# Per-head channel sums of an RWKV-7/HGRN2 layer as two rounded products instead of one float32 product, with the first tile's evacuation moved

## The chip, the cores and the metric

One Trainium2 chip, one NeuronCore. The metric is the device time of one execution in microseconds. The engines are TensorE (PE, with PEld for its weight loads), VectorE (DVE), ScalarE (ACT), GpSimd (POOL) and the DMA queues that SyncE (SP) issues.

## The reference

A trunk of two layers on 512 tokens of width 1024, all in float32. The change touches only the first ("even") layer, whose projection `z = h @ w_in` feeds eight HGRN2 heads of width 128 and sixteen RWKV-7 heads of width 64. Four values in it are sums over the channels of a head:

```
o  = rmsnorm(hgrn2(q, f, i))                      # mean of o*o over 128 channels
kk = k * k_k;  kk = kk / max(norm(kk), 1e-12)     # sum of kk*kk over 64 channels
y  = (y - mean(y)) * rsqrt(mean((y-mean(y))**2) + eps)   # sum of squares over 64 channels
y  = y + sum(r * k * r_k, -1) * v                 # the "bonus": sum over 64 channels
```

Then the outputs are gated, projected and added, and the second ("odd") layer (block attention and an RG-LRU) and a final norm follow.

## The kernel before

Channels lie on the 128 partitions and tokens along the free axis, so a tile of z is 128 x 512. Everything is written by hand for each engine, with semaphores between them.

The even layer runs in rounds. Round i projects eight tiles, `t(0)` to `t(7)`, that belong to HGRN2 head i and to the pair of RWKV-7 heads i. A tile is eight accumulated steps of 128 channels, and each step is three rounded (float32r) products, `split_products`: high weights by high input, high by low, low by high. A tile takes two weight units; POOL splits each unit into `w_hi` (line 352) and `w_lo` (line 354) into one of four slots (`split_unit`) once TensorE has left the slot (`units_done`). The tiles alternate between PSUM banks 0 and 1, and a bank must be emptied (`free0`, `free1`) before the tile after next starts in it; `gated(i, 0, ...)` on VectorE (line 1908) empties tile 0 by multiplying it with its sigmoid (`sig_q`, by ScalarE).

Between the tiles of round i TensorE computes HGRN2 head i (`hg_level`, `hg_diagonal`, `hg_keys`, `hg_changes`, `hg_outputs`) and the RWKV-7 pair r = i-1, whose tiles came in the round before. The pair starts with `low_rank(r)` at the head of the round; then, among `t(0)` and `t(1)`, stand the four channel sums: `key_norm(r)` and `hg_norm(r)` after the first half of `t(0)`, `head_var(r-1)` after its second half, `bonus(r)` after the first half of `t(1)`. Each is one float32 product of a 128 x 128 matrix of ones (`ones`) or of two 64 x 64 blocks of ones (`bones`) with a 128 x 512 operand:

```
mm(R0[:, :], bones, t1).then_inc(sem["rw_ssq"], 1)
```

After `t(2)` come `products(r)`, `turned_products(r)`, two `token_rows`, and the blockwise triangular inverse (`inverse_pt`, `inverse_n`), which runs between parts of `t(3)`.

VectorE's list at the head of round i is: `decay_sums(r)`, `key_norm(r)` (line 1990, a clamp of the sum, `rw_m1`), `operands(r)` (which waits for ScalarE's inverse root of it, `rw_rn`, and for the two exponentials), `read_operands(r)` (lines 2010 and 2011), `gated(i, 0)`, `head_norm`, `head_gate`, `pair_norm`, `pair_gain`, `pair_gate` (of pair r-1), `bonus`, then two tensor_scalars for the forget gates (lines 2158, 2159), `level(i, 0)`, `gated(i, 2)`, and the masked copies `strict` and `inverse_start` (line 1901), which `inverse_pt(r, 1, 0)` on TensorE waits for. Pair norm, gain and gate exist from round 2 on. `last_round` does the last pair (r = 7) between the embedding's and the output projection's tiles.

## Time and profile before

| | |
|---|---|
| median of 3 runs | 1178.47 us (1177.82 to 1179.08) |
| the profiled execution, its own time | 1178.48 us |
| its span in the trace | 1176.7 us |
| PE busy | 1144.8 us, 97% |
| DVE busy | 772.9 us, 66% |
| POOL busy | 635.8 us, 54% |
| ACT busy | 448.4 us, 38% |

The profiled execution lies on the median, and 1.8 us of its time are outside the span. The granted TensorE clock is 0.998 of full speed. Busy shares are means over the program: where an engine waits is read from its timeline. Matmuls overlap, so the time of one in a row of instructions is read from start to start.

### The profile page before, as it was taken

What the parts mean: (1) busy time and instruction counts of PE and PEld (TensorE: products, weight loads), DVE (VectorE), ACT (ScalarE), POOL (GpSimd) and SP (SyncE); (2) the same over time, 40 slices, a digit from 0 to 9 for tenths busy, and PEclk for the clock granted to TensorE, in tenths of its full rate; (3) what the DMA queues carried; (4) which work ended last, traced back from release to release, by engine and by line L of the source; (5) the groups of instructions that cost most, each with busy time, mean ns of one, the idle gap of its engine ahead of it and who ended that gap; (6) DMA issues with size and microseconds to landing.
All of it is one profiled execution on the core that took longest, in us unless ns stands there. A gap on an engine that the chain in (4) does not pass through costs nothing.

```text
span 1176.7 us, 31072 instructions
## 1 busy us (share of the span) xinstructions
PE 1144.8 (97%) x12076; PEld 906.7 (77%) x12076; DVE 772.9 (66%) x1350; ACT 448.4 (38%) x848; POOL 635.8 (54%) x594
## 2 busy tenths in 40 slices
PE   7899999999999999999999999999999999999996
PEld 4678877877788788777887778888777777778884
DVE  7874684675566756846755542539968686967647
ACT  5452343343433423433335420226234444352224
POOL 5553452443444534524435557777847475749872
PEclk9999999999999999999999999999999999999999
DMA  5221121211221212202212143333323232323331
GB/s 199 73 68 53 55 66 39 66 55 38 66 56 46 66 48 64 66 30 66 57 46 72 57 135 116 91 99 90 99 64 89 72 89 63 89 63 96 101 90 72
DMA packets 46890, 87.38 MB, mean 74 GB/s; under 512 B 5824, under 2 KB 7104, under 8 KB 46656
## 3 DMA queue, kind: packets, MB, share of 16 engines
q1 hardware_dynamic: 44496, 81.04, 23.6%
q10 hardware_dynamic: 2288, 4.72, 1.3%
q8 instruction: 91, 1.49, 0.5%
q14 instruction: 15, 0.12, 0.0%
HBM read 83.65 MB, written 2.10 MB: 73 GB/s over the span
## 4 chain that ended last, share of the span: by engine, by line
PE 86%; DVE 7%; issue 2%; ACT 1%; DVEq 0%; ACTq 0%
PE psum L398 83%; PE psum L1081 1%; DVE mix L1792 1%; DVE h_split L2399 1%; PE psum L552 1%; DVE y L1792 1%; ACT mix L1210 1%; DVE h_split L1792 1%; DVE mix L2578 0%; DVE psum L2335 0%; PE psum L714 0%; PE psum L550 0%; DVE mix L2343 0%; DVE mix L2574 0%; DVE psum L2350 0%
## 5 line engine op out<-in xcount | busy, mean ns | idle before, releaser
L398 PE MATMUL psum<-h_split,w_hi 128*128 128x512 f32 x2320 | 748.9, 404 | 14.0 <-DVE h_split L1792 9.0
L398 PEld LDWEIGHTS psum<-h_split,w_hi 128*128 128x128 f32 x2320 | 421.7, 188 | 118.2 <-issue 31.9
L352 POOL TENSOR_SCALAR w_hi<-w_raw 128x512 fp32r<-128x512 f32 x290 | 215.9, 745 | 480.5 <-PE psum L398 337.0
L398 PE MATMUL psum<-h_split,w_lo 128*128 128x512 f32 x1160 | 454.2, 392 | 0.0
L354 POOL TENSOR_TENSOR w_lo<-w_raw,w_hi 128x512 fp32r<-128x512 f32 x290 | 408.6, 1409 | 24.2
L398 PEld LDWEIGHTS psum<-mix 64*64 64x64 f32 (+3 forms) x8256 | 228.9, 138 | 69.1 <-issue 49.1
L1210 ACT ACTIVATE mix<-psum 128x512 f32<-128x512 f32 (+4 forms) x289 | 138.9, 494 | 368.9 <-PE psum L398 235.6
L398 PE MATMUL psum<-mix 64*64 64x64 f32 (+5 forms) x8256 | 269.6, 236 | 4.5 <-issue 2.6
L398 PEld LDWEIGHTS psum<-h_split,w_lo 128*128 128x128 f32 x1160 | 218.0, 188 | 48.2 <-issue 0.7
L1210 ACT ACTIVATE mix<-mix 128x512 f32<-128x512 f32 (+3 forms) x256 | 131.3, 546 | 119.8 <-DVE mix L2316 49.1
L1901 DVE COPY_PREDICATED mix<-mask,psum 128x128 f32<-128x128 uint8 (+1 forms) x192 | 82.0, 469 | 43.8 <-PE psum L398 41.5
L1210 ACT ACTIVATE mix<-psum,mix 128x512 f32<-128x512 f32 (+3 forms) x88 | 53.3, 630 | 98.4 <-PE psum L398 69.3
L1792 DVE SCALAR_TENSOR_TENSOR mix<-mix 128x512 f32<-128x512 f32 (+1 forms) x112 | 77.0, 688 | 14.9 <-ACT mix L1210 11.7
L1792 DVE SCALAR_TENSOR_TENSOR mix<-psum,mix 128x64 f32<-128x64 f32 (+1 forms) x80 | 37.3, 467 | 55.1 <-ACT mix L1210 46.0
L2050 DVE COPY mix<-psum 128x128 f32<-128x128 f32 (+1 forms) x80 | 25.5, 318 | 57.9 <-PE psum L398 57.6
L1210 ACT ACTIVATE h_split<-y 128x512 fp32r<-128x512 f32 x44 | 25.5, 627 | 69.9 <-PE psum L398 69.5
L398 PE MATMUL psum<-mix,fconst 128*128 128x512 f32 x92 | 45.4, 597 | 0.1
L1936 DVE TENSOR_TENSOR mix<-mix 128x256 f32<-128x256 f32 x56 | 36.1, 644 | 0.1
L2316 DVE TENSOR_TENSOR mix<-mix,psum 128x512 f32<-128x512 f32 x16 | 10.9, 679 | 24.8 <-PE psum L398 24.8
L1939 DVE TENSOR_TENSOR mix<-mix 128x256 f32<-128x256 f32 x56 | 27.0, 482 | 0.0
L2242 DVE TENSOR_TENSOR h_split<-y,h_split 128x512 fp32r<-128x512 f32 x10 | 11.5, 1206 | 23.4 <-ACT h_split L1210 23.4
L1796 DVE TENSOR_TENSOR h_split<-mix,h_split 128x512 fp32r<-128x512 f32 x16 | 18.6, 1163 | 12.4 <-ACT h_split L1210 12.4
(139 smaller groups left out, 709.7 us busy)
## 6 DMA issues: line engine op xcount, KB each, us to landing
w_raw<-wall SPq DMA_DIRECT2D x290, 256.0 KB, 2.6
mix<-xT SPq DMA_DIRECT2D x4, 512.0 KB, 7.1
mix<-xT ACTq DMA_DIRECT2D x1, 2048.0 KB, 8.1
out<-mix SPq DMA_DIRECT2D x7, 256.0 KB, 2.5
mix<-pT ACTq DMA_DIRECT2D x2, 512.0 KB, 3.9
mix<-lru_w ACTq DMA_DIRECT2D x4, 256.0 KB, 3.3
mix<-w2a ACTq DMA_DIRECT2D x16, 32.0 KB, 2.3
mask<-mask_u SPq DMA_DIRECT2D x1, 432.0 KB, 7.4
```

The source lines that it names most:

```text
L352: pool.tensor_scalar(w_hi[:, slot, :, :], w_raw[:, slot, :], 1.0, 0.0, ALU.mult, ALU.add).then_inc(sem["w_hi"], 1)
L354: pool.tensor_tensor(w_lo[:, slot, :, :], w_raw[:, slot, :], w_hi[:, slot, :, :].bitcast(F32).rearrange("p k n -> p (k n)"), ALU.subtract) ...
L398: return pe.matmul(o, lhsT, rhs, start=start, stop=stop, skip_group_check=True)
L552: last = pe.transpose(o[:, at], (b_t if n == 1 else k_t)[:, at], ident)
L1081: last = pe.transpose(bank[4][:, j * L:(j + 1) * L], prob[:, n % 2, j * L:(j + 1) * L], ident)
L1210: return act.activation(o, i, func, bias=bias, scale=scale, **kw)
L1792: return dve.scalar_tensor_tensor(out=o, in0=a, scalar=scalar, in1=b, op0=op0, op1=op1)
L1796: dve.tensor_tensor(h_split[:, KC + c, :], hn[:, c % 2, :], h_split[:, c, :].bitcast(F32), ALU.subtract).then_inc(sem["h_ready"], 1)
L1901: return dve.copy_predicated(dst, mask, src)
L1936: dve.tensor_tensor(q_dst, q_src, t_even.to_broadcast([P, nb, m]), ALU.mult)
L1939: dve.tensor_tensor(k_dst, k_src, t_odd.to_broadcast([P, nb, m]), ALU.mult)
L2050: dve.tensor_copy(dst, src).then_inc(sem["rw_pb"], 1)
```

## The change

It does these things:

- All four sums, in all eight pairs, become two rounded products each (`sum_products`): the operand's high half, rounded by ScalarE on its way into `sum_split`, and the low half, which POOL makes by a subtraction (`key_low`, `output_square_low`, `bonus_low`, `variance_low`). The variance and the bonus of the last pair stay single float32 products.
- ScalarE computes three of the operands twice, once in float32 and once rounded, and copies the fourth (`bonus_high`).
- `key_norm` moves on TensorE and on VectorE into the round before (after the first half of `t(7)`, and after the masked copies), and the logarithm and exponential behind it (`key_scale`) move on ScalarE ahead of the two decay exponentials.
- `gated(i, 0)` on VectorE moves ahead of `read_operands`.
- In `last_round` the output's sum moves between the two halves of the last tile.
- POOL's weight loop is unrolled to a whole round, with the subtractions at fixed places. One conversion of the constants (128 x 256) is added at the start.
- To make room, `t2`, `n_add`, `s_all` and `osig` share memory with other tiles, and two semaphores go.

```diff
+        sum_split = sb("sum_split", [P, 2, 2, T], F32R)
+        sum_const = sb("sum_const", [P, 2, P], F32R)
+        ones_r, bones_r = sum_const[:, 0, :], sum_const[:, 1, :]
...
-        t1, t2, w_a = (place(T) for _ in range(3))
+        t1, w_a = (place(T) for _ in range(2))
+        t2 = kr[:, 0, :]
...
-        n_add = place(T).rearrange("p (c t) -> p c t", c=RC)
-        s_all = place(T).rearrange("p (c t) -> p c t", c=RC)
+        n_add = k_t.rearrange("p (c t) -> p c t", c=RC)
+        s_all = b_t.rearrange("p (c t) -> p c t", c=RC)
...
+            def key_low(r):
+
+                pool.wait_ge(sem["sum_hi"], count("sum_hi", r, 0))
+                pool.tensor_tensor(sum_split[:, 0, 1, :], t1, sum_split[:, 0, 0, :].bitcast(F32), ALU.subtract).then_inc(sem["sum_lo"], 1)
...
+            def bonus_low(r):
+
+                pool.wait_ge(sem["sum_hi"], count("sum_hi", r, 2))
+                pool.tensor_tensor(sum_split[:, 0, 1, :], t2, sum_split[:, 0, 0, :].bitcast(F32), ALU.subtract).then_inc(sem["sum_lo"], 1)
+
+            def variance_low(r):
+
+                pool.wait_ge(sem["rw_dsq"], count("rw_dsq", r))
+                pool.tensor_tensor(sum_split[:, 1, 1, :], y_sq, sum_split[:, 1, 0, :].bitcast(F32), ALU.subtract).then_inc(sem["dsq_lo"], 1)
+
+            pool.wait_ge(const_loaded, 64)
+            pool.tensor_scalar(sum_const[:, :, :], fconst[:, 1:3, :], 1.0, 0.0, ALU.mult, ALU.add)
+
+            groups = 2 * TILES // SLOTS
...
+            key_low(0)
+            with pool.Fori(1, EV_ROUNDS) as i:
+                for g in range(groups):
+                    for slot in range(SLOTS):
+                        split_unit(i * groups + g, slot)
+                        if g == 0 and slot == 3:
+                            output_square_low(i - 1)
+                        elif g == 1 and slot == 0:
+                            bonus_low(i - 1)
+                        elif g == 3 and slot == 2:
+                            variance_low(i - 1)
+                key_low(i)
+            g_prj = (U_PRJ0 + 2) // SLOTS
+            for g in range(groups * EV_ROUNDS, g_prj):
+                for slot in range(SLOTS):
+                    split_unit(g, slot)
+            output_square_low(EV_ROUNDS - 1)
...
+            def sum_products(o, of, pair):
+
+                mm(o, of, sum_split[:, pair, 0, :], True, False)
+                return mm(o, of, sum_split[:, pair, 1, :], False, True)
+
             def low_rank(r):
                 pe.wait_ge(w2_loaded, (r + 1) * 32)
+                pe.wait_ge(sem["rw_m1"], count("rw_m1", r))
...
             def key_norm(r):
-                pe.wait_ge(sem["rw_ksq"], count("rw_ksq", r))
-                pe.wait_ge(sem["rw_sw"], count("rw_sw", r))
-                mm(R0[:, :], bones, t1).then_inc(sem["rw_ssq"], 1)
+                pe.wait_ge(sem["sum_lo"], count("sum_lo", r, 0))
+                sum_products(R0[:, :], bones_r, 0).then_inc(sem["rw_ssq"], 1)
 
             def head_var(r):
-                pe.wait_ge(sem["rw_dsq"], count("rw_dsq", r))
                 if isinstance(r, int) and r == EV_ROUNDS - 1:
+                    pe.wait_ge(sem["rw_dsq"], count("rw_dsq", r))
                     pe.wait_ge(sem["rw_s"], count("rw_s", r, 5))
+                    last = mm(R1[:, :], bones, y_sq)
                 else:
+                    pe.wait_ge(sem["dsq_lo"], count("dsq_lo", r))
                     pe.wait_ge(sem["rw_av"], count("rw_av", r + 1))
-                mm(R1[:, :], bones, y_sq).then_inc(sem["rw_var"], 1)
+                    last = sum_products(R1[:, :], bones_r, 1)
+                last.then_inc(sem["rw_var"], 1)
 
             def bonus(r):
-                pe.wait_ge(sem["rw_rk"], count("rw_rk", r))
-                pe.wait_ge(sem["rw_m1"], count("rw_m1", r))
-                mm(R0[:, :], bones, t2).then_inc(sem["rw_bon"], 1)
+                if isinstance(r, int) and r == EV_ROUNDS - 1:
+                    pe.wait_ge(sem["rw_rk"], count("rw_rk", r))
+                    pe.wait_ge(sem["rw_sw"], count("rw_sw", r))
+                    last = mm(R0[:, :], bones, t2)
+                else:
+                    pe.wait_ge(sem["sum_lo"], count("sum_lo", r, 2))
+                    pe.wait_ge(sem["rw_sw"], count("rw_sw", r))
+                    last = sum_products(R0[:, :], bones_r, 0)
+                last.then_inc(sem["rw_bon"], 1)
...
             def hg_norm(r):
-                pe.wait_ge(sem["hg_sq"], count("hg_sq", r))
-                mm(H0[:, :], ones, hk).then_inc(sem["hg_ssq"], 1)
+                pe.wait_ge(sem["sum_lo"], count("sum_lo", r, 1))
+                sum_products(H0[:, :], ones_r, 0).then_inc(sem["hg_ssq"], 1)
...
                 if pair:
-                    key_norm(r)
                     hg_norm(r)
                 t(0, 4, KC)
...
                 t(7, 0, 4)
+                key_norm(i)
                 hg_level(i, 6)
...
                 low_rank(r)
-                part_tile(EV_ROUNDS, 3, 0, KC)
-                key_norm(r)
+                part_tile(EV_ROUNDS, 3, 0, 4)
                 hg_norm(r)
+                part_tile(EV_ROUNDS, 3, 4, KC)
                 head_var(r - 1)
                 bonus(r)
...
             def out_squares(r):
                 act.wait_ge(sem["rw_yc"], count("rw_yc", r))
-                f(by_parity(y_sq.rearrange("p (c t) -> p c t", c=RC)),
-                  psum[:, 2:4, 256:512].rearrange("p g (c t) -> p g c t", c=4), ACT.Square).then_inc(sem["rw_dsq"], 1)
+                last = f(by_parity(y_sq.rearrange("p (c t) -> p c t", c=RC)),
+                         psum[:, 2:4, 256:512].rearrange("p g (c t) -> p g c t", c=4), ACT.Square)
+                if isinstance(r, int) and r == EV_ROUNDS - 1:
+                    last.then_inc(sem["rw_dsq"], 1)
+                else:
+                    if not is_first(r):
+                        act.wait_ge(sem["rw_var"], count("rw_var", r - 1))
+                    f(by_parity(sum_split[:, 1, 0, :].rearrange("p (c t) -> p c t", c=RC)),
+                      psum[:, 2:4, 256:512].rearrange("p g (c t) -> p g c t", c=4), ACT.Square).then_inc(sem["rw_dsq"], 1)
+
+            def key_scale(r):
+                act.wait_ge(sem["rw_m1"], count("rw_m1", r))
+                f(t1, t1, ACT.Ln).then_inc(sem["rw_ln"], 1)
+                act.wait_ge(sem["rw_ln"], count("rw_ln", r))
+                f(t1, t1, ACT.Exp, bias=bias[:, 2:3], scale=-0.5).then_inc(sem["rw_rn"], 1)
+
+            def bonus_high(r):
+                act.wait_ge(sem["rw_rk"], count("rw_rk", r))
+                act.wait_ge(sem["hg_ssq"], count("hg_ssq", r))
+                f(sum_split[:, 0, 0, :], t2, ACT.Copy).then_inc(sem["sum_hi"], 1)
...
                     act.preload_act_table_set("natural_log_exp_and_others")
+                    key_scale(r)
                     act.wait_ge(sem["rw_prep"], count("rw_prep", r, 0))
                     f(e_neg[:, :, 1:RL + 1], cum[:, :, 1:RL + 1], ACT.Exp, scale=KAPPA).then_inc(sem["rw_exp"], 1)
                     act.wait_ge(sem["rw_exp"], count("rw_exp", r, 0))
                     f(e_pos, cum, ACT.Exp, scale=-KAPPA).then_inc(sem["rw_exp"], 1)
                     if is_first(r):
                         decay_rates()
-                    act.wait_ge(sem["rw_m1"], count("rw_m1", r))
-                    f(t1, t1, ACT.Ln).then_inc(sem["rw_ln"], 1)
-                    act.wait_ge(sem["rw_ln"], count("rw_ln", r))
-                    f(t1, t1, ACT.Exp, bias=bias[:, 2:3], scale=-0.5).then_inc(sem["rw_rn"], 1)
+                    bonus_high(r)
                     act.wait_ge(sem["hg_ssq"], count("hg_ssq", r))
...
                 act.wait_ge(sem["free1"], freed(i, 5))
-                f(t1, wk, ACT.Square, scale=cur_e[:, K_K:K_K + 1]).then_inc(sem["rw_ksq"], 1)
+                f(t1, wk, ACT.Square, scale=cur_e[:, K_K:K_K + 1])
+                if pair:
+                    act.wait_ge(sem["rw_bon"], count("rw_bon", r))
+                f(sum_split[:, 0, 0, :], wk, ACT.Square, scale=cur_e[:, K_K:K_K + 1]).then_inc(sem["sum_hi"], 1)
...
                 f(hk, H1[:, :], ACT.Square).then_inc(sem["hg_sq"], 1)
+                act.wait_ge(sem["rw_ssq"], count("rw_ssq", i))
+                f(sum_split[:, 0, 0, :], H1[:, :], ACT.Square).then_inc(sem["sum_hi"], 1)
...
                     decay_sums(r)
-                    key_norm(r)
                     operands(r)
+                    gated(i, 0, "sig_q", sig_b, hq)
                     read_operands(r)
...
-                gated(i, 0, "sig_q", sig_b, hq)
+                if not pair:
+                    gated(i, 0, "sig_q", sig_b, hq)
...
                 masked(i, 7)
+                key_norm(i)
                 states(i)
```

VectorE at the head of a round from round 2 on, before. The `mix` tiles are all working tiles in SBUF; L1792 is a helper (scalar_tensor_tensor), L1990 is the clamp of the key sum, L2010 and L2011 are the read operands, L1908 is tile 0's evacuation; ISA and REGISTER_ALU rows are bookkeeping.

```order
184 L1792 SCALAR_TENSOR_TENSOR mix<-mix 128x512 [waits rw_prep]
185 L1990 TENSOR_SCALAR mix<-psum 128x512 [waits rw_ssq]
186 L1792 SCALAR_TENSOR_TENSOR mix<-mix 128x512 [waits rw_rn]
187 L2001 ISA
188 L1792 SCALAR_TENSOR_TENSOR mix<-mix 128x512 [waits rw_kk]
189 L2003 REGISTER_ALU
190 L2004 TENSOR_TENSOR mix<-mix 128x512 [waits rw_exp]
191 L2006 TENSOR_TENSOR mix<-mix 128x512 [waits rw_kk]
192 L2010 TENSOR_TENSOR mix<-mix 128x512
193 L2011 TENSOR_TENSOR mix<-mix 128x512
194 L1908 TENSOR_TENSOR mix<-psum,mix 128x512 [waits sig_q]
195 L1792 SCALAR_TENSOR_TENSOR mix<-psum,mix 128x512 [waits hg_rstd]
```

The same place in the change, where every line is 77 or 78 further down (L1869 is the helper, L2087 and L2088 the read operands, L1985 the evacuation).

```order
186 L1869 SCALAR_TENSOR_TENSOR mix<-mix 128x512 [waits rw_prep]
187 L1869 SCALAR_TENSOR_TENSOR mix<-mix 128x512 [waits rw_rn]
188 L2078 ISA
189 L1869 SCALAR_TENSOR_TENSOR mix<-mix 128x512 [waits rw_kk]
190 L2080 REGISTER_ALU
191 L2081 TENSOR_TENSOR mix<-mix 128x512 [waits rw_exp]
192 L2083 TENSOR_TENSOR mix<-mix 128x512 [waits rw_kk]
193 L1985 TENSOR_TENSOR mix<-psum,mix 128x512 [waits sig_q]
194 L2087 TENSOR_TENSOR mix<-mix 128x512
195 L2088 TENSOR_TENSOR mix<-mix 128x512
196 L1869 SCALAR_TENSOR_TENSOR mix<-psum,mix 128x512 [waits hg_rstd]
```

The clamp is gone from this place, and the evacuation with its wait for `sig_q` now stands ahead of the read operands; all that was behind it stands as it did.

ScalarE at the head of a round, before, from the first activation after its table load (L1210 is the helper for all activations) to the sigmoid of tile 0 (the last row).

```order
114 L1210 ACTIVATE mix<-mix 128x8x64 [waits rw_prep]
115 L1381 ISA
116 L1210 ACTIVATE mix<-mix 128x520 [waits rw_exp]
117 L1210 ACTIVATE mix<-mix 128x512 [waits rw_m1]
118 L1210 ACTIVATE mix<-mix,bias 128x512 [waits rw_ln]
119 L1210 ACTIVATE mix<-psum,bias 128x512 [waits hg_ssq]
120 L1210 ACTIVATE mix<-mix 128x512 [waits hg_ln]
121 L1210 ACTIVATE mix<-psum,bias 128x512 [waits rw_var]
122 L1210 ACTIVATE mix<-mix 128x512 [waits rw_lnv]
123 L1216 ISA
124 L1210 ACT_TABLE_LOAD
125 L1210 ACTIVATE mix<-psum 128x512 [waits units_done]
```

And in the change (the helper is L1269), up to the bookkeeping row ahead of the table load for the same sigmoid.

```order
119 L1269 ACTIVATE mix<-mix 128x512 [waits rw_m1]
120 L1269 ACTIVATE mix<-mix,bias 128x512 [waits rw_ln]
121 L1457 ISA
122 L1269 ACTIVATE mix<-mix 128x8x64 [waits rw_prep]
123 L1459 ISA
124 L1269 ACTIVATE mix<-mix 128x520 [waits rw_exp]
125 L1269 ACTIVATE sum_split<-mix 128x512 [waits hg_ssq,rw_rk]
126 L1269 ACTIVATE mix<-psum,bias 128x512 [waits hg_ssq]
127 L1269 ACTIVATE mix<-mix 128x512 [waits hg_ln]
128 L1269 ACTIVATE mix<-psum,bias 128x512 [waits rw_var]
129 L1269 ACTIVATE mix<-mix 128x512 [waits rw_lnv]
130 L1275 ISA
```

The pair of activations that waits for `rw_m1` now stands first, and one copy into `sum_split` is added behind the decay exponentials.

## Rows read from the trace of the kernel before

All groups but the first and the last are of round 5 of the even layer (pair 4), a round like every one from round 2 on.

**Rows 1.** The page, busy time, share and instructions of each engine.

```profile
PE 1144.8 (97%) x12076; PEld 906.7 (77%) x12076; DVE 772.9 (66%) x1350; ACT 448.4 (38%) x848; POOL 635.8 (54%) x594
```

**Rows 2.** Timeline, PE, around the channel sum `hg_norm`: start us, us, what.

```profile
400.81 0.40 PE L398 MATMUL psum<-h_split,w_lo 128*128 128x512 f32 x1
...
401.04 1.02 PE L398 MATMUL psum<-mix,fconst 128*128 128x512 f32 x2
...
402.37 0.39 PE L398 MATMUL psum<-h_split,w_lo 128*128 128x512 f32 x1
...
403.06 0.39 PE L398 MATMUL psum<-h_split,w_lo 128*128 128x512 f32 x1
```

**Rows 3.** Timeline, PE: `key_norm` with `hg_norm`, `products`, `inverse_pt`.

```profile
396.59 1.88 PE L398 MATMUL psum<-mix,fconst 128*128 128x512 f32 x4
...
413.81 2.66 PE L398 MATMUL psum<-mix 64*64 64x128 f32 x72
...
416.83 2.57 PE L398 MATMUL psum<-mix 64*64 64x64 f32 x128
```

**Rows 4.** Timeline, ACT, head of round 5: start, duration, idle before and releaser.

```profile
392.77 0.60 ACT L1210 ACTIVATE mix<-psum 128x512 f32<-128x512 f32 x1 [0.79 <-PE psum L398]
...
393.89 0.69 ACT L1210 ACTIVATE mix<-psum,mix 128x512 f32<-128x512 f32 x1 [0.52 <-PE psum L398]
...
395.21 1.28 ACT L1378 ACT_TABLE_LOAD   x1
...
396.51 1.30 ACT L1210 ACTIVATE mix<-mix 128x512 f32<-128x512 f32 x2
...
398.74 0.63 ACT L1210 ACTIVATE mix<-mix 128x512 f32<-128x512 f32 x1 [0.94 <-DVE mix L1990]
...
402.11 0.69 ACT L1210 ACTIVATE mix<-psum,bias 128x512 f32<-128x512 f32 x1 [0.73 <-PE psum L398]
...
404.77 0.60 ACT L1210 ACTIVATE mix<-psum 128x512 f32<-128x512 f32 x1
```

**Rows 5.** Timeline, DVE, head of round 5.

```profile
398.03 0.68 DVE L1990 TENSOR_SCALAR mix<-psum 128x512 f32<-128x512 f32 x1
...
400.16 1.48 DVE L1792 SCALAR_TENSOR_TENSOR mix<-mix 128x512 f32<-128x512 f32 x2 [1.46 <-ACT mix L1210]
...
402.58 1.78 DVE L2006 TENSOR_TENSOR mix<-mix 128x512 f32<-128x512 f32 x1
...
404.28 0.68 DVE L2010 TENSOR_TENSOR mix<-mix 128x512 f32<-128x512 f32 x1
...
405.49 0.68 DVE L1908 TENSOR_TENSOR mix<-psum,mix 128x512 f32<-128x512 f32 x1
...
406.97 1.00 DVE L1971 TENSOR_TENSOR y<-mix 128x512 f32 x1
...
412.01 1.64 DVE L2158 TENSOR_SCALAR mix<-mix 128x512 f32<-128x512 f32 x1
...
415.28 1.96 DVE L1901 COPY_PREDICATED mix<-mask,psum 128x256 f32<-128x256 uint8 x5
```

**Rows 6.** Timeline, POOL, head of round 5.

```profile
396.95 0.62 POOL L352 TENSOR_SCALAR w_hi<-w_raw 128x512 fp32r<-128x512 f32 x1 [3.62 <-PE psum L398]
...
402.20 1.61 POOL L354 TENSOR_TENSOR w_lo<-w_raw,w_hi 128x512 fp32r<-128x512 f32 x1
...
412.07 1.29 POOL L354 TENSOR_TENSOR w_lo<-w_raw,w_hi 128x512 fp32r<-128x512 f32 x1
```

**Rows 7.** Timeline, POOL and ACT, near tile 5 of round 5.

```profile
450.37 0.62 POOL L352 TENSOR_SCALAR w_hi<-w_raw 128x512 fp32r<-128x512 f32 x1 [2.83 <-PE psum L398]
...
456.19 0.72 ACT L1210 ACTIVATE mix<-mix 128x512 f32<-128x512 f32 x1
```

**Rows 8.** Timeline, PE: tile 2 of round 1, and `products` of the last round.

```profile
87.61 0.72 PE L398 MATMUL psum<-h_split,w_hi 128*128 128x512 f32 x2 [0.18 <-DVE mix L1908]
...
649.72 2.66 PE L398 MATMUL psum<-mix 64*64 64x128 f32 x72 [0.69 <-ACT mix L1210]
```

37 lines of the change are left out of this document (18 added, 19 removed).

## The prediction

> **What bounds the kernel now.** I read the page's busy line first: TensorE is busy 97% of the span, no other engine above 66% [rows 1]. So the span moves if TensorE has less to do, or if it must wait. The busy line can't say which, because the sums that shrink stand at the head of a round, where other engines feed TensorE. So I read, second, TensorE's timeline around one sum, to price it, and third the timelines of ScalarE, VectorE and GpSimd over the head of round 5, to see when each hands over and how far TensorE is from waiting. The reader is to see in them that TensorE has no gap there today, and that the first work to arrive close to TensorE's need is VectorE's masked copies, with under a microsecond to spare. The profiled execution took 1178.48 us (span 1176.7, 1.8 outside it), 0.01 from the median of the runs, so sums are made against 1178.5.
>
> **Price of a sum.** From the low-weight product ahead of `hg_norm` to the next one behind it, 400.81 to 402.37, is 1.56 us. That stretch holds the sum and one ordinary step of three products, and the next step takes 402.37 to 403.06, 0.69, or 0.23 a product [rows 2]. So the float32 sum costs 1.56 - 0.69 = 0.87 us, and its two rounded products 0.46: each sum gives back 0.41. Thirty of the thirty-two change (8 key, 8 output, 7 variance, 7 bonus): 30 x 0.41 = 12.3 us of TensorE work. The Trainium skill, FP8 and Floating Point Precision, TensorE Precision Notes, says that true float32 is four passes through the array; at four times 0.23 the sum would cost 0.92, and the gain would be 13.8. The row is the measurement, and the sum here goes by 0.87.
>
> Where this work lies matters. At the head of rounds 2 to 7 TensorE loses a whole key sum (0.87) and three times 0.41: 2.1 us. At the head of round 1 there is no variance: 0.87 + 0.82 = 1.69. In the last round the bonus stays, so 0.87 + 0.82 = 1.69 too. In exchange the key sum's two products are added in `t(7)` of eight rounds: 8 x 0.46 = 3.7 us. TensorE has no gap there to hide them.
>
> **Where TensorE would wait: `inverse_pt(r, 1, 0)`.** Today TensorE starts `products` at 413.81 and `inverse_pt` at 416.83 [rows 3]. The latter needs VectorE's first `strict` and `inverse_start`, the first two of the five masked copies that start at 415.28 and take 1.96 together [rows 5]; by their share I put the first two at 0.75 with the semaphore, 416.03. TensorE has 0.8 us to spare. With 2.1 us taken out ahead of it, it would arrive at 414.7, 1.3 before today's copies. So what the head of the round gives depends on how early the copies can come.
>
> ScalarE first. Its last square of the output starts at 392.77, and then it idles 0.52 for `low_rank` until 393.89; the added rounded square (as the first, 0.6) fits in that idle time but for under 0.1 [rows 4]. Sigmoids and the table load stay. The logarithm and exponential of the key sum move from 398.74 to the end of the load, 396.51, because the clamp is now a round old; the two decay exponentials (1.30 for both) follow. So the 0.94 us that ScalarE idled for the clamp is gone, and so is the 0.73 that it idled for `head_var`, which now comes with TensorE 1.7 us earlier [rows 4]. Against these stand `bonus_high`, a copy of 0.6, and the late start. Sum: 0.94 + 0.73 - 0.60 - 0.04 = 1.0 earlier, so the sigmoid of tile 0 moves from 404.77 to about 403.7, done at 404.35 [rows 4].
>
> VectorE next. It loses the clamp at 398.03 (0.68) and the idle 1.46 behind it [rows 5]. `operands`, which today run from 400.16 to 404.28 (4.1 us), then run from about 398.05 to 402.2. The evacuation of tile 0 needs the sigmoid and starts at 404.4. So VectorE idles some 2 us with the read operands (404.28 to 405.49, 1.2 us) behind the waiting instruction, where today they fill such time. From the evacuation to the masked copies VectorE takes 415.28 - 405.49 = 9.8 us today [rows 5]; now the read operands come on top: 404.4 + 9.8 + 1.2 = 415.4. That is 0.15 later than today, though everything ahead of it came earlier. Tile 0's bank is free by 405.1, and `t(2)` needs it at 413.81 - 2.1 less eight steps of 0.69, 406.2: no wait there [rows 2, 3].
>
> **GpSimd's part in it.** An SBUF-only instruction of VectorE that meets a GpSimd one is held: the operand multiply at 402.58 took 1.78 and ended 0.55 after GpSimd's subtraction (402.20 to 403.81), where the read operand at 404.28, with GpSimd idle, took 0.68; the forget gate at 412.01 took 1.64 across one of 1.29 [rows 5, 6]. The 9.8 us hold several of these, and the two read operands today hold none. With one more subtraction (`bonus_low`, 1.3 to 1.6 us, after the copy at about 399.8) ahead of the weight splits, and splits asked for earlier, the read operands would run into a split: at best 0, at worst about 0.9 in sum (each half a microsecond late). Copies then start 0.15 to 1.0 us after today's 415.28; nothing excludes either end, and I take the middle, 0.55. The Trainium skill, SBUF — State Buffer, Who interferes with whom, states the rule: a VectorE instruction with two SBUF inputs contends with a GpSimd instruction that reads SBUF, and whichever came first holds the other for its whole length. The trace agrees (402.58). By that rule alone each of the 31 added subtractions could hold VectorE by up to 1.3 us; most of them fall where VectorE has idle time.
>
> TensorE's saving at such a head is then 0.8 - 0.55 = 0.25 us instead of 2.1.
>
> **Sum.** Key products in eight rounds: +3.7. Round 1, where the pair norm, gain and gate do not exist yet and VectorE's list is three instructions shorter: the full -1.69, and the 0.18 that TensorE waited for tile 0's bank goes too [rows 8]: -1.9. Rounds 2 to 7: 6 x -0.25 = -1.5. Last round: today TensorE waits 0.69 for ScalarE's evacuation of an embedding tile ahead of `products` [rows 8]; that tile itself comes 1.7 earlier, and ScalarE's list is 1 us or more shorter ahead of it, so the whole -1.7. Total: 3.7 - 1.9 - 1.5 - 1.7 = -1.4 (the three fixed terms leave +0.1), so 1177.1 us. With copies at +0.15 it is 3.9 - 0.1 = 3.8 off (1174.7), with +1.0 it is 1.3 on (1179.8): this case's own range.
>
> **Edits at nothing.** The second squares of the variance and of the keys (0.6 and 0.7) push the next level copies on ScalarE by 1.3, which has waits for TensorE of that size behind them; without that cover it would be VectorE's level 7 and `hg_keys` that come late, 1.3 a round. `output_square_low`: the square is rounded by about 394.0, GpSimd is idle until 396.95 (idle 3.62 before it) [rows 4, 6], so the low half is there by 395.6 against TensorE's 396.59 [rows 3]. `bonus_low`: there by 401.4, needed two half tiles and two sums after 396.59, at 403.0. VectorE's clamp in its new place stands ahead of `states` in a wait for `hg_changes`. The constants' conversion, the memory moves and the two semaphores: nothing on any path that I read.
>
> **Rivals.**
> - *TensorE stays the bound.* If VectorE's blocked instructions come free as GpSimd's splits shift against them, the 9.8 us shrink; copies 1.3 us ahead of today's would reach all of it. For it: idle GpSimd leaves an instruction at 0.68 against 1.78. Against it: GpSimd has as many splits in the stretch as before. All of it gives 6 x -2.1 + 0.1 = -12.5, 1166.0; copies one microsecond ahead of today's 6 x -1.8 + 0.1 = -10.7, 1167.8; copies at today's time 6 x -0.8 + 0.1 = -4.7, 1173.8. This case spans 1166 to 1174.
> - *VectorE and GpSimd take turns (the slower side).* At the head of the round each SBUF-only instruction from the read operands on could find GpSimd ahead of it, at 1.3 us a time. With the copies at +1.5 each head of rounds 2 to 7 costs 0.7 more than today: 6 x 0.7 + 0.1 = 4.3, so 1182.8. It decides from +1.2 on (6 x 0.4 + 0.1 = 2.5).
> - *A low half or a split comes late.* GpSimd begins `variance_low` after the split that starts at 450.37, but the rounded square it needs follows the key square's place, 456.19 and on [rows 7]. So GpSimd stands over 4 us with one unit unsplit behind it. TensorE needs that unit only in the second half of `t(7)`, over 8 us on, so it should cost nothing; if GpSimd were late by 1 us in each of seven rounds, 1184.
>
> **How the numbers follow.** VectorE's list takes most of the gain (1174.7 to 1179.8): 0.60; TensorE stays the bound: 0.20; turns: 0.14; a late half: 0.06. No change within 0.2% is within 2.4 us, 1176.1 to 1180.9, about what a measurement can tell. In the first case the part under 1176.1 is a quarter and more, 0.17 of the 0.60. So faster 0.17 + 0.20 = 0.37, same 0.43, slower 0.20. The range leaves out the better part of the second case and the end of the third: 1169.5 to 1181.5.
>
> **What would show it.** In the changed kernel's trace: two rounded products of 0.23 where a sum was; ScalarE's tile 0 sigmoid 1 us earlier against `low_rank`; VectorE idle 1 to 2 us ahead of the evacuation; TensorE waiting 1 to 2 us ahead of `inverse_pt`, or `turned_products` held by the bonus, in rounds 2 to 7 and not in round 1; rounds as long as before. The prediction is wrong if no such wait shows and rounds are 1.6 us shorter, or if TensorE waits for a low half or for weights.

## The result, and the profile after

The changed kernel takes 1185.64 us (median of 6 runs, 1183.15 to 1187.98) against 1177.66 beside it: a ratio of 1.0067, interval 1.0055 to 1.0080. It is slower by 8 us, above the range of the prediction. The profiled execution took 1187.98 us, span 1186.2. Of all executions behind the times below one was slow, 1594.35 us at a granted clock of 0.657, of the version with the last round's sums as before; it is left out of that version's median.

The page's busy line of the changed kernel, to hold against [rows 1]:

```profile
PE 1140.1 (96%) x12076; PEld 909.5 (77%) x12076; DVE 813.1 (69%) x1350; ACT 462.9 (39%) x878; POOL 685.4 (58%) x625
```

TensorE has 4.7 us less to do, and the span is 9.5 longer. VectorE has as many instructions as before, 1350, and is busy 40 us longer. That is the line to stop at: the same instructions, held longer.

Where the time went is read from marks in TensorE's timeline of both kernels: `hg_values` and `hg_keys` of a HGRN2 head, and `token_rows` of the pair. A head is here what lies from `hg_keys` to the next `hg_values`. Against before, the changed kernel is 1.6 us later at the first `hg_values` (in an unaltered repeat 1.8, in the other versions from 0.3 earlier to 0.9 later, so not counted as the change's), 0.45 to 0.65 later in each of the eight stretches with `t(7)` (3.9 in sum), 0.4 earlier over the head of round 1, 2.8 later over the heads of rounds 2 to 7 (0.5 in a plain one, of it 0.18 ahead of `token_rows`; stalls of 0.7 to 1.6, which the trace puts down to issue, come and go there), 2.1 later over the last round up to `token_rows`, and 0.5 earlier behind it.

The head of round 5 after, to hold against [rows 3 to 6]. Timeline, PE: the two waits of the head, in `turned_products` and at `token_rows`.

```profile
418.61 1.56 PE L443 MATMUL psum<-mix 64*64 64x64 f32 x38 [1.11 <-DVE mix L2072]
...
421.15 0.65 PE L611 MATMUL psum<-fconst,mix 128*128 128x128 f32 x4 [0.75 <-DVE mix L1985]
```

Timeline, ACT: the output square, its rounded twin, and the sigmoid of tile 0.

```profile
397.44 0.60 ACT L1269 ACTIVATE mix<-psum 128x512 f32<-128x512 f32 x1 [0.79 <-PE psum L443]
397.93 0.59 ACT L1269 ACTIVATE sum_split<-psum 128x512 fp32r<-128x512 f32 x1
...
408.08 0.60 ACT L1269 ACTIVATE mix<-psum 128x512 f32<-128x512 f32 x1
```

Timeline, DVE: scan, `operands` (L2081, L2083), evacuation (L1985), `read_operands` (L2087, L2088), `head_gate` (L2048), `pair_gain`, bonus product (L2072), masked copies (L1978).

```profile
399.35 1.64 DVE L2055 TENSOR_TENSOR_SCAN mix<-mix 128x520 f32<-128x520 f32 x1 [0.71 <-ACT mix L1269]
...
401.40 5.12 DVE L1869 SCALAR_TENSOR_TENSOR mix<-mix 128x512 f32<-128x512 f32 x4
406.44 1.10 DVE L2081 TENSOR_TENSOR mix<-mix 128x512 f32<-128x512 f32 x1
407.46 1.78 DVE L2083 TENSOR_TENSOR mix<-mix 128x512 f32<-128x512 f32 x1
409.17 0.68 DVE L1985 TENSOR_TENSOR mix<-psum,mix 128x512 f32<-128x512 f32 x1
409.77 0.68 DVE L2087 TENSOR_TENSOR mix<-mix 128x512 f32<-128x512 f32 x1
410.37 1.77 DVE L2088 TENSOR_TENSOR mix<-mix 128x512 f32<-128x512 f32 x1
...
412.95 1.59 DVE L2048 TENSOR_TENSOR y<-mix 128x512 f32 x1
...
415.17 1.77 DVE L1869 SCALAR_TENSOR_TENSOR mix<-mix 128x512 f32<-128x512 f32 x1
...
417.88 0.68 DVE L2072 TENSOR_TENSOR mix<-psum,mix 128x512 f32<-128x512 f32 x1
...
421.01 1.95 DVE L1978 COPY_PREDICATED mix<-mask,psum 128x256 f32<-128x256 uint8 x5
```

Timeline, POOL: splits (L357, L359), and `bonus_low` (L390).

```profile
402.65 1.61 POOL L359 TENSOR_TENSOR w_lo<-w_raw,w_hi 128x512 fp32r<-128x512 f32 x1
404.36 1.61 POOL L390 TENSOR_TENSOR sum_split<-mix,sum_split 128x512 fp32r<-128x512 f32 x1
405.95 1.06 POOL L357 TENSOR_SCALAR w_hi<-w_raw 128x512 fp32r<-128x512 f32 x1
407.09 1.60 POOL L359 TENSOR_TENSOR w_lo<-w_raw,w_hi 128x512 fp32r<-128x512 f32 x1
408.66 1.06 POOL L357 TENSOR_SCALAR w_hi<-w_raw 128x512 fp32r<-128x512 f32 x1
409.81 1.78 POOL L359 TENSOR_TENSOR w_lo<-w_raw,w_hi 128x512 fp32r<-128x512 f32 x1
```

Count from the output square. Before: evacuation 405.49 - 392.77 = 12.72 behind it, copies 22.51. After: evacuation 11.73, copies 23.57. The evacuation came forward by 1.0, and what lies between it and the copies grew from 9.79 to 11.84, two read operands included. They are all of the growth: from the first one's start to the next instruction they take 2.29 (409.77 to 412.06), where they took 1.21, and what is left is 0.24 shorter than before (9.55 for 9.79). VectorE is not idle ahead of the evacuation. Four of its instructions around and behind it take 1.6 to 1.8, and each overlaps a low half of GpSimd. TensorE has to wait twice, 1.11 for VectorE's bonus product and 0.75, at `token_rows`, for the evacuation of tile 2.

The last round, TensorE's first product of the embedding, GpSimd's subtraction that it needs, and the windows behind (the third number from the end is the granted clock):

```profile
650.33 0.74 PE L443 MATMUL psum<-h_split,w_hi 128*128 128x512 f32 x2 [2.07 <-issue]
```

```profile
647.74 2.49 POOL L368 TENSOR_TENSOR h_split<-mix,h_split 128x512 fp32r<-128x512 f32 x2 [5.53 <-ACT h_split L1269]
```

```profile
650.20:652.20 2.00, 1.87 (x6) 1.52 (x7) 1.51 (x2) 0.45 (x1) 1.92 (x4) 0.66 0.00 0
652.20:654.20 2.00, 2.00 (x6) 1.60 (x5) 2.00 (x3) 0.60 (x1) 1.92 (x2) 0.50 0.41 78
654.20:656.20 2.00, 2.00 (x10) 1.57 (x9) 0.14 (x1) 1.24 (x2) 0.68 (x1) 0.99 0.22 77
```

TensorE stands 2.07 us until GpSimd has subtracted, and then runs some 4 us at half its clock (1.2 GHz). The trace puts the wait down to issue; the subtraction ends 0.1 ahead of the product, so it is the subtraction's.

### The profile page after: what moved, and what is told of

It is laid out like the page before. It is cut to its first block, busy times and chain, and to the rows that moved or that the text cites. A ratio compares the mean times of both kernels' runs of the same rounds, so it can differ in the third digit from the quotient of the medians.

```text
span 1186.2 us, 31073 instructions
## 1 busy us (share of the span) xinstructions
PE 1140.1 (96%) x12076; PEld 909.5 (77%) x12076; DVE 813.1 (69%) x1350; ACT 462.9 (39%) x878; POOL 685.4 (58%) x625
## 4 chain that ended last, share of the span: by engine, by line
PE 73%; DVE 16%; issue 5%; ACT 2%; DVEq 0%; ACTq 0%
PE psum L443 70%; DVE mix L1869 4%; ACT mix L1269 1%; DVE mix L2088 1%; PE psum L1140 1%; DVE mix L2083 1%; PE psum L611 1%; DVE mix L1985 1%; DVE h_split L2477 1%; DVE y L1869 1%; DVE mix L2081 1%; DVE h_split L1869 1%; DVE mix L2236 1%; DVE mix L2656 0%; DVE psum L2413 0%
## 5 line engine op out<-in xcount | busy, mean ns | idle before, releaser
L357 POOL TENSOR_SCALAR w_hi<-w_raw 128x512 fp32r<-128x512 f32 x290 | 224.7, 775 | 400.5 <-PE psum L443 268.1
L359 POOL TENSOR_TENSOR w_lo<-w_raw,w_hi 128x512 fp32r<-128x512 f32 x290 | 410.2, 1415 | 24.2
L1269 ACT ACTIVATE mix<-psum 128x512 f32<-128x512 f32 (+4 forms) x289 | 139.5, 494 | 384.9 <-PE psum L443 192.7
L1269 ACT ACTIVATE mix<-mix 128x512 f32<-128x512 f32 (+3 forms) x256 | 131.3, 547 | 107.4 <-DVE mix L2394 47.9
L1978 DVE COPY_PREDICATED mix<-mask,psum 128x128 f32<-128x128 uint8 (+1 forms) x192 | 81.7, 470 | 45.4 <-PE psum L443 42.9
L1869 DVE SCALAR_TENSOR_TENSOR mix<-mix 128x512 f32<-128x512 f32 (+1 forms) x112 | 92.5, 832 | 3.2
L1269 ACT ACTIVATE mix<-psum,mix 128x512 f32<-128x512 f32 (+3 forms) x88 | 53.2, 629 | 91.9 <-PE psum L443 63.0
L1869 DVE SCALAR_TENSOR_TENSOR mix<-psum,mix 128x64 f32<-128x64 f32 (+1 forms) x80 | 37.5, 468 | 46.4 <-ACT mix L1269 37.9
L1269 ACT ACTIVATE h_split<-y 128x512 fp32r<-128x512 f32 x44 | 25.5, 626 | 69.8 <-PE psum L443 69.4
L2013 DVE TENSOR_TENSOR mix<-mix 128x256 f32<-128x256 f32 x56 | 38.4, 686 | 0.1
L2016 DVE TENSOR_TENSOR mix<-mix 128x256 f32<-128x256 f32 x56 | 31.0, 554 | 0.0
L2017 DVE TENSOR_TENSOR mix<-mix 128x256 f32<-128x256 f32 (+6 forms) x56 | 30.1, 537 | 0.0
L395 POOL TENSOR_TENSOR sum_split<-mix,sum_split 128x512 fp32r<-128x512 f32 x7 | 9.1, 1299 | 31.1 <-ACT sum_split L1269 31.1
```

The source lines that it names most:

```text
L357: pool.tensor_scalar(w_hi[:, slot, :, :], w_raw[:, slot, :], 1.0, 0.0, ALU.mult, ALU.add).then_inc(sem["w_hi"], 1)
L359: pool.tensor_tensor(w_lo[:, slot, :, :], w_raw[:, slot, :], w_hi[:, slot, :, :].bitcast(F32).rearrange("p k n -> p (k n)"), ALU.subtract) ...
L1269: return act.activation(o, i, func, bias=bias, scale=scale, **kw)
L1869: return dve.scalar_tensor_tensor(out=o, in0=a, scalar=scalar, in1=b, op0=op0, op1=op1)
L1978: return dve.copy_predicated(dst, mask, src)
L2013: dve.tensor_tensor(q_dst, q_src, t_even.to_broadcast([P, nb, m]), ALU.mult)
```

## The experiments

Each run stands beside runs of the kernel before on the same chip: 1178.44 us for the first four, 1177.81 for the next four, 1178.61, 1178.06 and 1178.37 for the rest.

**The changed kernel again**, unaltered.

> The changed kernel, unaltered, on the chip of the three experiments beside it. All theories expect it slower than before by 0.5 to 0.9%; it is the reference of the others. Its profile also tells whether the start repeats: in the first profile a product took 0.42 us until 15 us into the span where before it did so only until 11 us, which was worth 1.6 us. If that is the change's doing, it repeats.

1186.16 us, ratio 1.0066 (1.0051 to 1.0080). The loss holds, and from round 3 on evacuation and copies of every head are the same to 0.02 us.

**Last round's sums as before.** `hg_norm` behind the whole last tile, output and variance sum there in float32:

```
-                part_tile(EV_ROUNDS, 3, 0, 4)
-                hg_norm(r)
-                part_tile(EV_ROUNDS, 3, 4, KC)
+                part_tile(EV_ROUNDS, 3, 0, KC)
+                hg_norm(r)
```

> The changed kernel with the three sums of the last round (output, variance, bonus) as single float32 products again and the output's sum behind the whole of tile 3, as before; GpSimd's subtractions stay. Theory (the embedding's split bounds the last round, and the idle gap costs TensorE its clock): from the end of tile 3 to the first embedding tile is 3.6 us whatever TensorE does in it, because ScalarE and GpSimd split the embedding in that time; so the slower sums cost nothing there, the output's sum leaves the path (0.46 us), the gap shrinks from 2.07 to about 1.0 us, the granted clock stays full over the first embedding tiles (1.6 us): 2.1 us faster than the changed kernel. Rival (TensorE's own work bounds the last round): 3 x 0.41 = 1.2 us slower.

1184.66 us, 1.0058 (1.0043 to 1.0073). The last round is 1.7 us shorter than in the changed kernel in the profile (its clock stays at 1.00 and the empty stretch is 1.22); the medians show 1.5, at the edge of what they tell.

**Read operands first**, as before:

```
-                    gated(i, 0, "sig_q", sig_b, hq)
                     read_operands(r)
+                    gated(i, 0, "sig_q", sig_b, hq)
```

> The changed kernel with the read operands ahead of tile 0's evacuation again, as before. Theory (GpSimd's instructions hold VectorE's operands until after the sigmoid is there, so nothing waits at the evacuation): the order of the two is worth nothing, within 1 us of the changed kernel; the evacuation comes 1.2 to 2.4 us later, and TensorE may wait up to 0.8 us a round for bank 0 ahead of tile 2, which only shortens its wait ahead of the turned products. Rival (the evacuation's wait for the sigmoid holds the read operands up, as the prediction had it): copies 1.2 us earlier in each of six rounds, up to 7 us faster.

1188.53 us, 1.0083 (1.0062 to 1.0104), 2.4 above the changed kernel; neither theory had it slower. In round 1 TensorE waits 2.11 for tile 0's bank, the granted clock is 0.50 from 90 to 92 us, behind that wait, and `token_rows` comes 2.6 later; in rounds 2 to 7 TensorE waits 1.6 to 1.8 for that bank, no longer for the bonus and tile 2's, and `token_rows` comes 0.4 earlier. So the moved evacuation is worth its place in round 1 and costs a little in the others.

**Without GpSimd's low halves** (all four `_low` calls out; TensorE takes the high half twice, so every rounded sum is a rounded value doubled):

> The changed kernel without GpSimd's low halves: its 31 subtractions are left out and each second product of a sum takes the high half again, so the sums are not those of the reference; TensorE, ScalarE and VectorE have the same instructions in the same order. Theory (the added subtractions hold VectorE's two-input instructions at the head of the round, and VectorE then holds TensorE): the operands stage on VectorE, 7.8 us from the first to the evacuation in the changed kernel, falls by 1.5 to 3 us, the masked copies come 1 to 2 us earlier, and six to seven rounds save 1 to 1.7 us each: 6 to 12 us faster than the changed kernel, level with the kernel before or below it. Rival (ScalarE's longer list sets the evacuation, and with it the copies): within 2 us of the changed kernel.

1182.75 us, 1.0039 (1.0024 to 1.0055): 3.4 below the changed kernel, where 6 to 12 were expected. Round 1's head gives its 2.1, but the heads of rounds 2 to 7 only 0.4 against the changed kernel, with GpSimd doing what it did before. At that point my theory was that VectorE's list is simply as long as a head, and that the key sum's 0.47 in `t(7)` is what is lost. The next four runs were made to test it.

**Key sum unmoved**: the float32 key sum with its clamp, logarithm and exponential where they stood; output, variance and bonus rounded; last round as before. In even rounds:

```
                 if pair:
+                    key_norm(r)
                     hg_norm(r)
...
                 t(7, 0, 4)
-                key_norm(i)
```

> The kernel before with three sums rounded and nothing moved: output sum (rounds 1 to 7), bonus (rounds 1 to 7) and variance (rounds 2 to 7) are two rounded products each; the key sum stays one float32 product after the first half of t(0), its clamp, logarithm and exponential stand where they stood, the read operands stand ahead of the evacuation, and the last round's sums are float32 behind the whole last tile. 20 sums of 0.41, so 8.2 us of TensorE work less, and nothing added in t(7). Theory (the move of the key sum costs 0.47 a round in t(7) because TensorE has no gap there, and gives nothing back because VectorE's list ends last at the head of rounds 2 to 7; the last round lost some 2 us by a moved sum and an empty stretch): with both undone, 8 x 0.47 and the 2 us are gone, TensorE reaches inverse_pt 1.23 earlier against 0.8 of spare time, and the copies come 0 to 0.5 later by GpSimd's two added subtractions: 0.3 to 0.8 less a round in rounds 2 to 7, 0.8 in round 1, so 1173 to 1176 us. Rival (the added work on ScalarE and GpSimd is what makes the heads long): heads of rounds 2 to 7 stay 0.2 longer than before, so 1179 to 1180.

1193.13 us, 1.0116 (1.0088 to 1.0145): 17 us and more beyond the theory, and slower than the changed kernel. **The same with the evacuation first in round 1 alone**:

> As the run with the key sum in its old place, but in round 1 alone the evacuation of tile 0 stands ahead of the read operands, as in the changed kernel. Theory (in round 1 TensorE waited 2.11 us for tile 0's bank where the read operands stood first): TensorE comes 0.8 earlier to that bank than before, where it waited 0.18, so the wait without the move is about 1.0, and with it none: 0.5 to 1.0 us faster than the run beside it, all of it ahead of round 1's value projection. Rival (in round 1 the copies end last too): the same time within 0.3.

1189.52 us, 1.0096 (1.0066 to 1.0126). Up to `token_rows` round 1 is 1.0 shorter, as expected; much of the rest of the distance is rounds 5 and 6, where `token_rows` came 2.5 late in the one and 0.9 in the other, for no difference in the code.

The traces show why both are slow. VectorE's evacuation of tile 0, behind its operands and the read operands, comes 15.53 behind the output square in round 5 of the first version (12.72 before), and TensorE stands 1.8 for that bank in the heads of rounds 3 to 7, 2.03 in round 2. In some heads the granted clock then falls to half. The same round 5, the wait and the windows behind it (the third number from the end is the granted clock):

```profile
415.93 0.73 PE L435 MATMUL psum<-h_split,w_hi 128*128 128x512 f32 x2 [1.81 <-DVE mix L1983]
```

```profile
416.00:418.00 2.00, 2.00 (x7) 1.63 (x8) 1.85 (x3) 0.51 (x1) 1.13 (x1) 0.76 0.42 120
418.00:420.00 2.00, 2.00 (x6) 1.52 (x6) 1.80 (x4) 0.00 (x0) 0.00 (x0) 0.50 0.37 131
```

It fell in rounds 2, 5, 6 and 7 of the first version and in rounds 2 and 7 of the second. In these rounds `token_rows` comes 2.5 to 2.7 later than before, in the other ones of rounds 2 to 7 0.9. So rounds 5 and 6 differ by the clock.

**Moves only**: every sum float32, all moves kept.

> The changed kernel with every sum a single float32 product: only the moves are left (key sum in t(7), its clamp, logarithm and exponential early, tile 0's evacuation ahead of the read operands, the last round's output sum between the halves of the last tile). GpSimd's subtractions, ScalarE's second squares and its copy are out. TensorE's work is that of before; 8 float32 key sums of 0.87 stand in t(7) instead of at the heads. Theory (a head of rounds 2 to 7 is as long as VectorE's list, and the moves don't shorten that list): each round is 0.87 longer in t(7) and its head is not shorter than in the kernel before but by the 0.3 or less that VectorE gains where GpSimd has nothing added; round 1 gives 0.9 back, the last round costs 1 to 2: 1178.4 + 7.0 - 0.9 - 0 to 2 + 1 to 2, so 1184 to 1187. Rival (the moves do bring the list forward, and the added work on GpSimd and ScalarE ate it in the changed kernel): each head gives its 0.87 back, so 1178 to 1180.

1181.16 us, 1.0025 (1.0013 to 1.0037). Up to `token_rows` the head of each of rounds 2 to 7 is 0.91 shorter, each stretch with `t(7)` 0.86 longer: there the moves give back what they take. Of the 3.4 us that are left 0.8 is the last round; the rest is not placed. The theory said 1184 to 1187.

**Key and variance rounded, output and bonus float32**, all moves kept:

```
             def hg_norm(r):
-                pe.wait_ge(sem["sum_lo"], count("sum_lo", r, 1))
-                sum_products(H0[:, :], ones_r, 0).then_inc(sem["hg_ssq"], 1)
+                pe.wait_ge(sem["hg_sq"], count("hg_sq", r))
+                mm(H0[:, :], ones, hk).then_inc(sem["hg_ssq"], 1)
```

> The changed kernel, with output and bonus sums back to single float32 products: ScalarE's rounded output square and bonus copy and GpSimd's two subtractions for them are out; the key and variance sums stay rounded, and all moves stay. TensorE has 15 x 0.41 = 6.2 us more to do, all at the heads of rounds and in the last one. Theory (TensorE waits 1.1 and 0.75 at the heads of rounds 2 to 7 for VectorE's list): the added 0.82 a head is hidden in those waits, and the list is 0.4 or so earlier without the subtraction and the copy (the run without any low halves showed 0.4): heads of rounds 2 to 7 0.2 to 0.5 shorter than in the changed kernel, round 1 0.4 to 0.8 shorter or even, last round 0.4 longer: 1183 to 1185. Rival (the precision of these two sums is worth their 0.41 each): 1186.1 + 6, so 1190 to 1192.

1175.24 us, 0.9975 (0.9957 to 0.9992): faster than both kernels, 11 us below the changed one with 6 us more TensorE work. Up to `token_rows` the heads of rounds 2 to 7 are 1.30 shorter than before, the full 0.87 + 0.41. My theory fell, and so did its rival.

**The same with the last round's sums behind the tile**:

> The version with only key and variance sums rounded, and in the last round hg_norm behind the whole last tile and pair 6's variance as one float32 product. Theory (in the last round TensorE has an empty stretch ahead of the first embedding tile, and a sum placed there is free): 0.9 us less than the version without it, 1174.3 us. Rival (the stretch is not empty there): the same or 0.4 longer, 1175.2 to 1175.6.

1174.64 us, 0.9965 (0.9952 to 0.9978). The last round is 0.7 us shorter in the trace; the medians cannot tell it. It is the base of the runs that follow.

**GpSimd's subtractions alone**, over constants, nobody waiting for them:

```
+                pool.wait_ge(sem["hg_sq"], count("hg_sq", r))
+                pool.tensor_tensor(sum_split[:, 0, 1, :], flat_const, flat_const, ALU.subtract)
```

> The kernel of the run beside it (key and variance rounded, last round's sums behind the tile) with two GpSimd subtractions of constants a round added where output_square_low and bonus_low stand, 128 x 512 each, waiting for the same squares and operands; nobody waits for them, and neither ScalarE nor TensorE has anything more to do. Theory A (GpSimd's added subtractions make the head long: they hold VectorE, and the one for the bonus pushes the weight splits together so that they meet VectorE's whole list behind the evacuation): copies 1.0 to 1.4 later than in the run beside it, TensorE's spare time there is 0.5 or so, 0.5 to 1.0 a head, 3 to 6 us in all: 1177 to 1180. Theory B (ScalarE's added square and copy and TensorE's waits for the low halves do it, and GpSimd only fills idle time): the same time within 1 us.

1176.62 us, 0.9985 (0.9970 to 0.9999). Heads of rounds 3 to 7 are up to `token_rows` as in the base, to 0.01: the 2 us that VectorE idles ahead of the evacuation take the subtractions up. Only round 2 is 2.1 longer, as much as the 2.0 between the medians: there a split's low half starts 3.55 behind the evacuation, VectorE's `head_gate` 3.79, and the gate takes 1.59, as in the changed kernel. Theory A's 0.5 to 1.0 a head is not there.

**Output rounded too, and bonus rounded too**, each alone on the base.

> As the run with key and variance rounded and the last round's sums behind the tile, and the output sum of rounds 1 to 7 rounded too (7 x 0.41 = 2.9 us of TensorE work less, one square more on ScalarE, one subtraction more on GpSimd, ahead of the splits). Theory A: the subtraction meets only the scan (0.4 later), which VectorE's idle 2 us ahead of the evacuation takes up, and it doesn't delay a split; TensorE comes 0.4 earlier to the copies: between nothing and the full 2.9, so 1171.5 to 1174.5. Theory C (TensorE's coming earlier draws the weight splits forward into VectorE's list, as where the low halves were left out): the head is longer by 0.5 or more, 1177 or more.

> As the run with key and variance rounded and the last round's sums behind the tile, and the bonus sum of rounds 1 to 7 rounded too (2.9 us of TensorE work less, one copy more on ScalarE ahead of the head's exponentials, one subtraction more on GpSimd between two weight splits). Theory A: the subtraction delays the splits behind it until they run without a gap, the copy delays tile 0's sigmoid by 0.6 less what ScalarE idles: 0.5 to 1.5 a head, 1177 to 1183. Theory B (only the output's early square and subtraction harm, as they hold the scan at the head of VectorE's list): between nothing and the full 2.9 off, 1171.5 to 1174.5.

Output: 1172.88 us, 0.9949 (0.9934 to 0.9965), heads 0.38 shorter than the base, the fastest kernel of this study. Bonus: 1183.04 us, 1.0039 (1.0024 to 1.0055), heads 1.5 longer though TensorE has 0.41 less to do. So one sum, the bonus, costs 8.4 us, and neither GpSimd's subtractions by themselves (2.0) nor a third rounded sum (1.8 gained) does. VectorE's and GpSimd's timelines at the head of round 5 show how. The base:

```profile
399.23 0.69 DVE L1979 TENSOR_TENSOR mix<-psum,mix 128x512 f32<-128x512 f32 x1 [1.99 <-ACT mix L1266]
399.84 1.53 DVE L2081 TENSOR_TENSOR mix<-mix 128x512 f32<-128x512 f32 x1
...
402.79 0.79 DVE L2042 TENSOR_TENSOR y<-mix 128x512 f32 x1
...
404.21 1.06 DVE L1863 SCALAR_TENSOR_TENSOR mix<-mix 128x512 f32<-128x512 f32 x1
405.44 0.87 DVE L1863 SCALAR_TENSOR_TENSOR y<-mix 128x512 f32 x1 [0.16 <-DVE mix L1863]
...
406.83 0.92 DVE L2230 TENSOR_SCALAR mix<-mix 128x512 f32<-128x512 f32 x1
```

```profile
399.54 1.28 POOL L359 TENSOR_TENSOR w_lo<-w_raw,w_hi 128x512 fp32r<-128x512 f32 x1
...
403.12 1.61 POOL L359 TENSOR_TENSOR w_lo<-w_raw,w_hi 128x512 fp32r<-128x512 f32 x1
...
405.86 1.60 POOL L359 TENSOR_TENSOR w_lo<-w_raw,w_hi 128x512 fp32r<-128x512 f32 x1
```

and with the bonus rounded:

```profile
403.18 0.68 DVE L1982 TENSOR_TENSOR mix<-psum,mix 128x512 f32<-128x512 f32 x1
...
406.96 1.58 DVE L2045 TENSOR_TENSOR y<-mix 128x512 f32 x1
...
410.09 1.53 DVE L1866 SCALAR_TENSOR_TENSOR y<-mix 128x512 f32 x1 [0.16 <-DVE mix L1866]
...
412.15 1.59 DVE L2233 TENSOR_SCALAR mix<-mix 128x512 f32<-128x512 f32 x1
```

```profile
406.71 1.29 POOL L359 TENSOR_TENSOR w_lo<-w_raw,w_hi 128x512 fp32r<-128x512 f32 x1
...
409.39 1.69 POOL L359 TENSOR_TENSOR w_lo<-w_raw,w_hi 128x512 fp32r<-128x512 f32 x1
...
412.19 1.27 POOL L359 TENSOR_TENSOR w_lo<-w_raw,w_hi 128x512 fp32r<-128x512 f32 x1
```

In the base `head_gate` (L2042; L2045 in the other) starts at 402.79, the low half at 403.12: the gate takes 0.79, and GpSimd's instruction is drawn out from 1.28 to 1.61. With the bonus rounded the low half starts at 406.71, `head_gate` at 406.96, and the gate takes 1.58. From there on VectorE's list is late, and the next two splits hold it too: three meetings of the two engines have turned over. The splits are released by TensorE, which is 0.41 ahead; VectorE's list is released by ScalarE's sigmoid, which is not. (With the output rounded it is: `head_var` comes 0.4 earlier, and ScalarE, which idled 0.52 for it in the base, follows.) Four of the last five runs test that phase.

**Two more products ahead of the bonus's two** (their result is overwritten):

```
+                    mm(R0[:, :], bones_r, sum_split[:, 0, 0, :])
+                    mm(R0[:, :], bones_r, sum_split[:, 0, 0, :])
                     last = sum_products(R0[:, :], bones_r, 0)
```

> The kernel with key, variance and bonus rounded (1183.0 us), with two more rounded products put ahead of the bonus's two, over the same high half, their result overwritten. TensorE's work at the bonus is then 0.9 us again, as with one float32 product; ScalarE's copy and GpSimd's subtraction stay. Theory C (phase: GpSimd's weight splits follow TensorE, VectorE's list follows ScalarE's sigmoid of tile 0; rounding the bonus brings the splits 0.35 ahead against VectorE's list, so that from the second split after the evacuation on each finds VectorE at a start instead of in the middle, and five of its instructions take 1.5 to 1.8 instead of 0.7 to 1.1): with TensorE back in step the splits fall as with key and variance alone (3.9 us behind the evacuation instead of 3.5), copies 10.45 behind it instead of 12.2, and 7 x 0.46 more TensorE work makes the kernel faster: 1174 to 1176. Theory A (the added subtraction and the added copy themselves make the head long): 1183 or more, up to 1186.

1179.19 us, 1.0015 (1.0001 to 1.0029), 3.9 us less than without the added work (3.3 with each held against the runs beside it). `head_gate` takes 0.69, the copies come 10.57 behind the evacuation. It misses the 1174 to 1176 of the theory: round 2 still falls the bad way at the last split (copies 11.67), and the start and plain stretches of this profile are a microsecond or so longer.

**The bonus without its subtraction** (high half twice, so the bonus is a rounded value doubled), **and with the high half made by VectorE** instead of ScalarE:

```
-                    bonus_high(r)
...
+                    stt(sum_split[:, 0, 0, :], wr, cur_r[:, R_K:R_K + 1], k_t, ALU.mult, ALU.mult).then_inc(sem["sum_hi"], 1)
                     stt(t2, wr, cur_r[:, R_K:R_K + 1], k_t, ALU.mult, ALU.mult).then_inc(sem["rw_rk"], 1)
```

> The kernel with key, variance and bonus rounded (1183.0 us), without GpSimd's subtraction for the bonus: TensorE takes the high half twice, so the bonus is a rounded value doubled. TensorE's work and ScalarE's copy are the same. Theory C (phase): the splits come as early against VectorE's list or earlier, so the copies stay 11.5 or more behind the evacuation: 1179 to 1183. Theory A (the subtraction makes the head long): the head is 0.4 shorter than with key and variance alone: 1172 to 1174.5.

> The kernel with key, variance and bonus rounded (1183.0 us), with the bonus's high half made by VectorE (the same product written a second time, rounded, 0.9 to 1.7 us in the 2 us that VectorE idles ahead of the evacuation) instead of ScalarE's copy; GpSimd's subtraction stays. Theory C (phase): ScalarE waits for head_var as with key and variance alone, so the evacuation doesn't move, and TensorE behind the bonus is 0.41 ahead: the splits meet VectorE as in the kernel with the copy, 1180 to 1184. Theory B (ScalarE's copy, which fills ScalarE's idle time ahead of head_var, makes the head long): 1172 to 1174.

1184.07 us, 1.0049 (1.0033 to 1.0066), and 1188.76 us, 1.0086 (1.0065 to 1.0107). Both lie above what the phase had promised (1179 to 1183, 1180 to 1184). Taking GpSimd's part away gains nothing: VectorE idles its 2 us again and the evacuation is where the base has it, but the low half still starts 0.05 ahead of `head_gate`. Taking ScalarE's away costs 5.7 more. VectorE has a longer list and its idle time was gone (evacuation 12.04 behind the square instead of 11.40), which is 0.3 a head in rounds 2 to 7 and 1.3 in round 1 up to `token_rows`; the other 2.6 lie behind `token_rows` and are not placed. So GpSimd's subtraction is out as a rival. ScalarE's copy is out less by its own run, which added work to VectorE, than by three others: with it the evacuation comes 0.03 later than in the base (11.40 for 11.37), and the padded and the nudged version keep it and have shorter heads.

**One more GpSimd instruction**, ahead of the split that meets `head_gate`:

```
+                        elif g == 1 and slot == 2:
+                            pool.tensor_scalar(sum_split[:, 1, 1, :], fconst.rearrange("p n t -> p (n t)"), 1.0, 0.0, ALU.mult, ALU.add)
```

> The kernel with key, variance and bonus rounded (1183.0 us), with one more GpSimd instruction a round (a conversion of constants, 128 x 512, 0.6 to 1.0 us, which nobody reads) ahead of the split whose low half began 3.53 us behind the evacuation, so that this low half begins at 4.1 or later, behind the start of head_gate at 3.8. TensorE, ScalarE and VectorE have the same work. Theory C (phase): head_gate takes 0.7 to 1.1 instead of 1.58, the copies come up to 0.9 earlier, up to 0.9 a head: 1177 to 1180; but the two splits behind it are released by TensorE as before, and if they meet VectorE at its starts all the same, the head gets back only a part: up to 1183. Theory A (GpSimd's amount of work makes the head long): more work, so 1183 or more, 1184 to 1187.

1181.30 us, 1.0018 (1.0005 to 1.0030). The low half starts 4.13 behind the evacuation, `head_gate` takes 0.80 and each head of rounds 3 to 7 is 0.53 shorter up to `token_rows`, with more work on GpSimd and the same elsewhere. The times alone would not show it: against the runs beside them they are 1.5 us apart, and the intervals overlap. The last split still meets VectorE (an instruction of 1.64), which the expectation left open.

**The last round's rounded sum behind the whole tile**:

> The changed kernel, with only hg_norm of the last round moved behind the whole last tile (its sums stay rounded). TensorE's empty stretch ahead of the first embedding tile, 2.07 us there, becomes 1.6. In the changed kernel the granted clock fell to 0.5 to 0.7 behind that stretch. Theory D (it is the empty stretch's length that brings the lower clock): no dip, 0.46 less by the moved sum and 1.6 less by the clock, 1184. Rival (the dip is not tied to the stretch: it came and stayed away at the same 2.07): 1185.7, with a dip or without.

1187.33 us, 1.0081 (1.0049 to 1.0112). The last round is 0.1 shorter, and the granted clock falls all the same (0.55 and 0.60 in the two windows behind the stretch). The stretch measured 2.01, not 1.6: the embedding's first product came 0.4 later behind the tile (GpSimd's two subtractions ahead of it took 2.89 instead of 2.49), so the run did not make the stretch shorter, and it doesn't decide between theory D and its rival.

All runs at the head of round 5, worked out from their timelines (us behind the evacuation; the last two columns: copies behind the output square, and how much later than in the kernel before `token_rows` comes behind that square):

| kernel | first three low halves start | `head_gate` starts, takes | copies | from square | head |
|---|---|---|---|---|---|
| key, var + moves (base) | 0.31 3.89 6.63 | 3.56, 0.79 | 10.45 | 21.81 | -1.31 |
| moves only | 0.30 3.88 6.62 | 3.55, 0.78 | 10.44 | 22.21 | -0.91 |
| base + GpSimd load | 0.40 3.89 6.63 | 3.65, 0.70 | 10.46 | 21.82 | -1.30 |
| base + output | 0.42 3.89 6.63 | 3.67, 0.69 | 10.46 | 21.45 | -1.68 |
| base + bonus, padded | 0.65 3.95 6.75 | 3.79, 0.69 | 10.57 | 21.99 | -1.19 |
| base + bonus, nudged | 0.65 4.13 6.84 | 3.78, 0.80 | 11.68 | 23.09 | -0.31 |
| without low halves | 0.02 3.21 5.95 | 3.27, 1.78 | 11.89 | 23.17 | -0.22 |
| base + bonus, no low half | 0.31 3.50 6.24 | 3.55, 1.78 | 12.18 | 23.55 | +0.17 |
| changed kernel | 0.64 3.53 5.93 | 3.78, 1.59 | 11.84 | 23.57 | +0.18 |
| base + bonus | 0.64 3.53 6.21 | 3.78, 1.58 | 12.20 | 23.60 | +0.21 |
| base + bonus by VectorE | 0.64 3.54 5.94 | 3.78, 1.59 | 11.84 | 23.88 | +0.50 |

Read the second against the third column: where the second low half starts behind `head_gate`, by 0.16 or more, the gate takes 0.7 to 0.8; where it starts ahead of it, if only by 0.05, 1.6 to 1.8.

## Why the prediction was wrong, step by step

- **Price of a sum.** Right. Two rounded products take 0.47 from start to start in the last tile (643.56 to 644.03), and a head with key and variance changed is 1.30 shorter, 0.87 + 0.41. The key sum's +3.7 in `t(7)` was 3.9. The subtractions added are 30, not 31; the other added GpSimd instruction is the constants' conversion.
- **ScalarE.** Right: the sigmoid of tile 0 comes 1.36 nearer to the output square (10.64 instead of 12.00); 1.0 was said.
- **VectorE idles some 2 us ahead of the evacuation.** Wrong for the changed kernel, where `operands` end only at the evacuation: the scan was held 0.4 by `output_square_low`, four instructions 0.9 by GpSimd, `operands` 1.1 more. Right for the base, to 0.01 (1.99). I had counted GpSimd's contention on the read operands alone.
- **Rounds 2 to 7, "I take the middle, 0.55": -0.25 each.** This step failed. The copies came 1.06 later, just beyond the bound of +1.0, and a plain head became 0.5 longer, not 0.25 shorter: over the six heads 2.8 lost in the profile, where the sum had 1.5 gained. The term that was mis-sized is the read operands behind the evacuation, put at 1.2 with 0 to 0.9 for splits that they meet; they took 2.29. Behind it stood a wrong picture: I let "GpSimd has as many splits in the stretch as before" stand for the same cost. The cost depends on which of the two starts first at each meeting, and TensorE's own saving moves that: its sums shrank, the splits came 0.35 to 0.4 ahead against VectorE's list. Against the base two meetings turned over in the changed kernel, at `head_gate` (1.59 for 0.79) and `pair_gain` (1.77 for 1.06). The wait also came earlier than at `inverse_pt`: 1.11 for the bonus, which is named among the signs, and 0.75 for tile 2's bank, which is not.
- **Round 1: -1.9.** Measured -0.4. The evacuation's move did what was said (without it 2.11 of wait, half the clock behind the wait, and 2.6 over the head), but TensorE waited 1.26 ahead of `token_rows` for VectorE there too; without low halves the head gave 2.1.
- **Last round: -1.7.** Measured +2.1, a miss of 3.8, next to the 4.3 of the six heads the largest. I took ScalarE's evacuation for the limit and did not ask what the sums at the end of the tile were covering. From the tile's end to the first embedding product it takes 3.58 before and 3.56 after: ScalarE's split and GpSimd's 2.5 us of subtraction, both behind the tile. Before, four float32 sums filled it. The output's was moved into the tile, where it costs 0.47, the key's into the round before, and the variance's shrank; nothing could be gained, and the 2.07 left empty were followed by half the clock, some 1.6 us (pairs of products 1.05 instead of 0.62). With the sums back in place the round is within 0.4 of before (last sums float32), 0.2 on the base.
- **Rivals.** "VectorE and GpSimd take turns" named the mechanism, with a chance of 0.14. That its price, 1182.8, comes within 3 us of the 1185.6 measured is in part luck: it stood for copies at +1.5, they came at +1.06, and the last round's loss is in none of the cases. The added subtractions by themselves cost nothing in a plain round (the load run). "TensorE stays the bound" is what happens without the bonus. "A low half comes late" did not occur: TensorE never waits for one.

The rule of the Trainium skill, SBUF — State Buffer, Who interferes with whom (a VectorE instruction with two SBUF inputs contends with GpSimd's read, and issue order decides who is blocked for the whole instruction), is borne out by the table. The prediction quoted it and used it to bound the added subtractions, where it should have been laid over the splits that were there already. VectorE's instruction with one input in PSUM takes 0.67 to 0.70 in every run (`tensor_tensor`, 128 x 512), whatever GpSimd does, as that section has it.

What stays open: when the granted clock falls behind a wait of TensorE and when not. In the last round it fell behind an empty stretch of 2.07 in the changed kernel and of 2.01 with the sum behind the tile, and it stayed at 1.00 behind 2.07 in the run without low halves and in the one with key and variance rounded. In the key-unmoved versions it fell behind some waits of 1.81 to 2.03, and not behind others of 1.81 to 1.83 nor behind one of 2.31 in round 1.

## What to carry to other kernels

When two engines hold each other up, as VectorE and GpSimd do here, and each is released by a different third one, a saving on the releasing engine shifts one list against the other, and a shift of 0.2 us (a low half 0.16 behind `head_gate` or 0.05 ahead of it) goes with 1.4 a head; lay the two lists side by side at the new offset before believing a saving. Test such a change one part at a time: of four sums here three gain 5.7 us with their moves and the last round's sums behind its tile, and the fourth turns that into a loss. And before moving or shrinking work that stands ahead of a wait, ask what the wait is for: there it was free. A wait can cost more than its length: in the key-unmoved versions half the clock behind 1.8 us of it took another 1.6 (2.5 for 0.9).

## What the runs showed that was not expected

More work made the kernel faster twice: two idle products a round on TensorE gave 3.9 us (1183.04 to 1179.19), one instruction on GpSimd 0.53 us a head. Rounds lock: from round 3 on, evacuation and copies repeat from round to round to 0.05 us in every version with the key sum moved, so a bad meeting is paid in each round alike. And the same code in the same place can cost 1.6 us more in one round than in another, when the clock falls behind a wait (the two key-unmoved versions).
